# Length of queries and keys in the token stage: a sum onto all partitions and a wide root and inverse, in place of a narrow sum, a narrow root and a spread

## The chip, the core and the metric

The kernel runs on one core of a Trainium2 chip. The metric is the device time of one execution in microseconds, of which three are given for the kernel before. Engines are named as in the profile: PE is TensorE (matmul) and PEld its weight load, DVE is VectorE, ACT is ScalarE, POOL is GpSimd, SP is SyncE, whose queue issues most of the DMAs. Each engine takes its instructions in the order in which they were written for it, and waits at semaphores.

## The reference, cut to what matters

Two transformer layers are followed by a third block with a gated delta rule and sixteen experts. The change lies in that third block, where the tokens' queries, keys and values are made. There are 512 tokens, four heads and 128 features a head:

```python
def l2norm(x):
    xf = x.astype(jnp.float32)
    return xf * lax.rsqrt(jnp.sum(xf * xf, axis=-1, keepdims=True) + EPS)
...
    proj = h @ w_in
    (q, k, v), log_a, beta = deltanet_inputs(proj[..., :QKV_COLS], proj[..., QKV_COLS:STATE_COLS],
                                             conv_w, a_log, dt_bias)
    q = l2norm(q) * DN_HEAD_DIM ** -0.5
    k = l2norm(k)
    o, states = bidir_delta(q, k, v, log_a, beta, s0)
```

`deltanet_inputs` runs a convolution of four taps along the tokens over each feature and then silu. `l2norm` divides each token's 128 features of one head by their length.

## The kernel before, in words

The stage is the class `Mixer2`, "token stage" below. Activations lie transposed: 128 features on the partitions, 512 tokens along the free axis. Tile c (0 to 11) is one head of the queries (0 to 3), keys (4 to 7) or values (8 to 11). Tiles 0 to 7 are divided by their length, tiles 8 to 11 are not.

The stage's matmuls come in 20 items (`self.items`), each with half a block of `win2`. Items 0 to 3, 6 to 9 and 12 to 15 make tiles 0 to 3, 4 to 7 and 8 to 11, 24 matmuls of 512 columns each; items 4, 5, 10 and 11 make the gate and 16 to 19 the pool's input, 48 matmuls of 256 columns each. A product is taken in three parts, high by high, high by low and low by high, so ACT first rounds an item's weights ("split", line 490, CAST 128x1024) and DVE subtracts for the low part (line 264, TENSOR_TENSOR 128x1024). At step i, splits are made mostly for item i + 3.

The generator `steps` sets the order. All engines run through the same list of (name, number) and each does its part of a step, so the list is the order of every queue. Per step i:

- PE: item i, then "finish", then "csum" where they stand.
- ACT: copies the product out of its bank (line 840, `put_act`; for other items lines 280 and 3125), casts the next split, and in `conv_act` takes the tanh for the silu and, for tiles 0 to 7, the square.
- DVE: the low part of the split, "finish", then `conv_dve`: one TENSOR_SCALAR and three SCALAR_TENSOR_TENSOR for the taps, and after ACT's tanh one more for the silu.

"conv" of tile c stands at the item's own step from c = 2 on. Its first tap overwrites the buffer `ctmp[c % 2]`, which holds the squares of tile c - 2.

The length is found like this. "csum" of tile c: four matmuls, each with 128 tokens of the squares as weights and a column of ones, leave the sums with tokens on the partitions, 4 columns a tile, in bank 6. "root", once for four tiles: DVE adds the epsilon and takes the inverse of 128x16 numbers (line 885), ACT takes their root. "finish" of tile c: four matmuls with a column of the roots repeated 128 times as weights and the identity spread them over all partitions into bank 2 or 3, and DVE multiplies the tile by that bank (line 274, from PSUM). Csum stands at steps 2 to 5 and 8 to 11, root at steps 5 and 11, finish of tiles 0 to 3 at steps 6 to 9 and of tiles 4 to 7 at steps 12 to 15.

Between them stand "delta" 0 to 3 at steps 2 to 5 (narrow work on the decays; the last has 34 matmul records on PE), "gate" 0 to 3 at steps 11 to 14 (a tanh on ACT and one operation on DVE each), and at steps 14, 16 and 18 a CAST of 128x2048 on ACT for the pool (line 3013). The stage ends with transposes ("turn", line 388) and the pool's matmuls.

Of the kernel before, what the change touches and what calls it, by code (L numbers as in the profile page):

```python
# [11 lines left out]
ACT = mybir.ActivationFunctionType  # L12
# [10 lines left out]
EPS = 1e-6  # L23
# [229 lines left out]
def mm(e, out, l, r, start=True, stop=True):  # L253
    return e.h.matmul(out, l, r, start=start, stop=stop)  # L254
# [2613 lines left out]
class Mixer2(Conv):  # L2868


    def __init__(self, k):
        super().__init__(k, "mixb", "mixb")
        al = k.al
        k.reset()
        self.nt = 4
        self.qkf = al(4096)
        self.qT, self.kT = v3(self.qkf[:, 0:2048], 4), v3(self.qkf[:, 2048:4096], 4)
        self.gate, self.ab = v3(al(2048), 4), v3(al(64), 4)
        vTf, tmpf = al(2048), al(2048)
        self.vT = self.O = v3(vTf, 4)  # L2880
        self.poolT = v3(tmpf, 4)
        self.utf, self.rawf = al(2048), al(2064)
        self.ut, self.mT, raw = v3(self.utf, 4), v3(self.rawf[:, 0:2048], 4), v3(self.rawf, 4)
        self.poolw = al(512)
        self.uhi4 = k.fr(tmpf).rearrange("p (g t c) -> p t g c", g=4, t=4)
        self.ulo4 = k.fr(self.utf).rearrange("p (t g c) -> p t g c", g=4, t=4)
        self.inv = v3(k.b4f, 4)
        self.Kt, self.Vt = v3(k.low[:, 0:2048], 4), v3(k.low[:, 2048:4096], 4)
        self.units()
        self.hp = k.parts(k.hTf, k.low)  # L2890
        self.conv_init(raw, 512, [tmpf[:, 512 * i:512 * i + 512] for i in range(4)], 0,
                       lambda i: (self.qT, self.kT, self.vT)[i // 4][:, i % 4, :],
                       lambda i: (128.0 ** -0.5, 1.0, None)[i // 4])
        self.dma, self.dma_inv = k.count("in_poolw"), k.count("in_inv")
        self.items = []
        w = k.A["win2"]
        for blk, kind in ((0, "fm"), (1, "fm"), (6, "gate"), (2, "fm"), (3, "fm"), (7, "gate"), (4, "fm"), (5, "fm"),
                          (8, "ut"), (9, "ut")):
            self.add("fm" if kind == "fm" else "tok", w[blk], SLOT, (kind, blk))
        self.number()  # L2900
        self.last_gate = max(i for i, it in enumerate(self.items) if it.tag[0] == "gate")
        self.nbox = k.ring.reserve(4)
        self.bx = [v3(k.fr(k.ring.slot(self.nbox + g)), 4) for g in range(4)]
        self.ends = [(self.V, "O"), (self.S, ("mT", 3)), (self.P, ("pool", 3))]
# [8 lines left out]
    def steps(self):  # L2913
        yield from self.first()
        yield "norm", 0
        pend, fin = [], []
        for i, it in enumerate(self.items):
            open_ = [j for j in (i - 1, i) if j >= 0 and (self.items[j].kind == "tok" and not self.items[j].half) == (j < i)]
            for j in open_:
                if j < i and j + 3 < len(self.items):  # L2920
                    yield "split", j + 3
            yield "sum", i
            if i in open_ and i + 3 < len(self.items):
                yield "split", i + 3
            if i == 1:
                yield "small", 0
                yield "conv", 0
            elif i == 2:
                yield "small", 1
                yield "conv", 1  # L2930
            if 2 <= i < 6:
                yield "delta", i - 2
            if fin:
                yield "finish", fin.pop(0)
            if pend and pend[0][1] + 2 <= i:
                c = pend.pop(0)[0]
                yield "csum", c
                if c % 4 == 3:
                    yield "root", c // 4
                    fin = [c - 3, c - 2, c - 1, c]  # L2940
            if it.tag[0] == "fm":
                c = self.conv_of(i)
                if c > 1:
                    yield "conv", c
                if self.scale(c) is not None:
                    pend.append((c, i))
            g = i - 11
            if 0 <= g < 4:
                yield "gate", g
        for c in fin:  # L2950
            yield "finish", c
        for m in range(8):
            yield "turn", m
        yield "O", 0
        for g in range(4):
            yield "box", g
            if g:
                yield "pool", g - 1
        yield "pool", 3
# [5 lines left out]
    def tok_pe(self, e, i, bank, src, ready):  # L2965

        half = self.items[i].half
        for a in range(2):
            j = i - half + a
            hi, lo, _ = self.views(j)  # L2970
            e.wait_ge(self.lower(j).at(("lo", j)))
            for t in range(2):
                c = slice((2 * half + t) * 128, (2 * half + t) * 128 + 128)
                for k in range(4):
                    x = src(4 * a + k)
                    e.wait_ge(ready(4 * a + k))
                    p = mm3(e, bank[:, 256 * t:256 * t + 256], (x[0][:, c], x[1][:, c]), (hi[:, k, :], lo[:, k, :]),
                            a == 0 and t == 0 and k == 0, a == 1 and t == 1 and k == 3)
            p.then_inc(*self.P.tick((("half", "sum")[a], i)))

    def conv_of(self, i):
        it = self.items[i]
# [37 lines left out]
    def pe(self, e):  # L3020
        k, P, S, V, B = self.k, self.P, self.S, self.V, self.k.bank
        self.enter(e)
        for name, i in self.steps():
# [4 lines left out]
            elif name == "sum" and i > 1:  # L3028
                it = self.items[i]
                if it.kind == "fm":  # L3030
                    c = self.conv_of(i)
# [6 lines left out]
                        e.wait_ge(V.at(("ulo", old[-1])) if self.items[old[-1]].tag[0] == "ut" else S.at(("tok", old[-1])))  # L3038
                    self.tok_pe(e, i, B[it.half], self.hp, lambda c: V.at(("h", c)))
            elif name == "csum":  # L3040
                e.wait_ge(V.at("small_tr") if i < 4 else V.at(("cmean", i // 4 - 1)))
                self.csum_pe(e, i, B[6])
            elif name == "finish":
                if i >= 2:
                    e.wait_ge(V.at(("cfin", i - 2)))
                self.finish_pe(e, i, B[2 + i % 2])
            elif name == "small":
                if i:
                    self.small_tr_pe(e, B[6], 4)
                else:  # L3050
                    self.small_pe(e, B[7], 2, 512, self.hp)
            elif name == "delta":
                e.wait_ge(V.at("small"))
                self.delta.pe_step(e, self.delta.SETUP[i], 0)
            elif name == "turn":
                if i < 4:
                    e.wait_ge(V.at(("ulo", len(self.items) - 1)))
                else:
                    e.wait_ge(S.at(("raw", 11)))
                if i >= 6:  # L3060
                    e.wait_ge((S if i % 2 else V).at(("turn", i - 6)))
                src, _ = self.turn(i)
                for c in range(4):
                    e.wait_ge(self.conv_done(4 + 4 * (i // 4) + c))
                    p = k.tr(e, B[i % 6][:, c * 128:c * 128 + 128], src[c])
                p.then_inc(*P.tick(("turn", i)))
            elif name == "box":
                n = self.nbox + i
                a = 2 * (i % 2)
                e.wait_ge(S.at(("bx", i)), V.at(("ulo", len(self.items) - (3 if i < 2 else 1))))  # L3070
                if i >= 2:
                    e.wait_ge(S.at(("mT", i - 2)))
                else:
                    e.wait_ge(S.at(("turn", 7)), V.at(("turn", 6)))
                self.box_pe(e, i, B[a], self.bx[i]).then_inc(*P.tick(("box", i)))
                k.ring.released[n] = [(P, ("box", i))] + (self.delta.ends if i >= 2 else [])
            elif name == "pool":
                b = 2 * (i % 2) + 1
                e.wait_ge(S.at(("mT", i)), self.dma.at(0))
                if i >= 2:  # L3080
                    e.wait_ge(V.at(("pool", i - 2)))
                mm(e, B[b][:, :], self.poolw[:, i * 128:i * 128 + 128], self.mT[:, i, :]).then_inc(*P.tick(("pool", i)))
# [15 lines left out]
    def act(self, e):  # L3098
# [4 lines left out]
        for name, i in self.steps():  # L3103
# [22 lines left out]
                if i in (14, 16, 18):  # L3126
                    self.box_act(e, i // 2 - 7)
            elif name == "root":
                self.croot_act(e, i)
            elif name == "conv":  # L3130
                self.conv_act(e, i)
            elif name == "gate":
# [14 lines left out]
    def dve(self, e):  # L3147
        k, P, S, V, B = self.k, self.P, self.S, self.V, self.k.bank
        self.enter(e)
        e.h.memset(self.raw[:, :, 0:2], 0.0)  # L3150
        e.h.memset(self.raw[:, :, 514:516], 0.0).then_inc(*V.tick("zero"))
        for name, i in self.steps():
            if name == "split":
                self.split_dve(e, i)
            elif name == "norm":
# [3 lines left out]
                for c in range(9):  # L3159
# [5 lines left out]
                    if c:  # L3165
# [1 line left out]
                        e.wait_ge(S.at(("nhi", c - 1)))  # L3167
                        stt(e, lo, k.two[(c - 1) % 2], k.MOD[:, c - 1, 0:1], hi.bitcast(F32), ALU.add, ALU.subtract).then_inc(
                            *V.tick(("h", c - 1)))
            elif name == "root":  # L3170
                self.croot_dve(e, i, B[6])
            elif name == "finish":
                self.finish_dve(e, i, B[2 + i % 2])
            elif name == "delta":
                e.wait_ge(V.at("small_tr"))
                self.delta.dve_step(e, self.delta.SETUP[i], 0)
# [884 lines left out]
```

## Time and profile before

| | before |
|---|---|
| three executions, us | 2977.16, 2980.09, 2974.94; median 2977.16 |
| profiled execution, us | 2971.13 |
| its span, us | 2969.3 |
| mean granted clock of PE | 0.989 |
| busy share of PE, DVE, ACT, POOL | 96%, 55%, 34%, 9% |
| HBM read | 436.40 MB |

The span is what the hardware profiler recorded from the first to the last instruction; the execution's own time is 1.8 us longer. A matmul that waits in PE's pipe counts as busy, so 96% doesn't say that PE is at its peak. The share of an engine is a mean over stages with different limits. The token stage takes from 2133 to 2299 us of the span.

### The profile page before, as it was taken

What the parts mean: (1) busy time and instruction counts of PE and PEld (TensorE: products, weight loads), DVE (VectorE), ACT (ScalarE), POOL (GpSimd) and SP (SyncE); (2) the same over time, 40 slices, a digit from 0 to 9 for tenths busy, and PEclk for the clock granted to TensorE, in tenths of its full rate; (3) what the DMA queues carried; (4) which work ended last, traced back from release to release, by engine and by line L of the source; (5) the groups of instructions that cost most, each with busy time, mean ns of one, the idle gap of its engine ahead of it and who ended that gap; (6) DMA issues with size and microseconds to landing.
All of it is one profiled execution on the core that took longest, in us unless ns stands there. A gap on an engine that the chain in (4) does not pass through costs nothing.

```text
span 2969.3 us, 41268 instructions
## 1 busy us (share of the span) xinstructions
PE 2838.8 (96%) x17052; PEld 2193.0 (74%) x17052; DVE 1624.5 (55%) x3042; ACT 1012.9 (34%) x2075; POOL 258.3 (9%) x284
## 2 busy tenths in 40 slices
PE   8999999999999999999999999999999897998888
PEld 6888877888888888888887888888788885332323
DVE  6876686465655565555585565454555764221213
ACT  4222363563332343232353552222344552000002
POOL 0000012230000000000022330000000730000000
PEclk9999999999999999999999999999999998999999
DMA  5454421112232222222221112222322028999997
GB/s 204 181 207 162 181 102 57 44 72 99 94 116 89 99 86 93 83 82 86 86 86 44 57 67 104 100 85 93 110 72 85 3 102 324 413 424 425 425 425 323
DMA packets 59868, 444.58 MB, mean 150 GB/s; under 512 B 6816, under 2 KB 7072, under 8 KB 23072
## 3 DMA queue, kind: packets, MB, share of 16 engines
q1 hardware_dynamic: 56544, 430.12, 37.7%
q0 software_dynamic: 1696, 6.55, 0.6%
q10 hardware_dynamic: 1440, 5.25, 0.5%
q8 instruction: 135, 2.21, 0.3%
q14 instruction: 53, 0.43, 0.0%
HBM read 436.40 MB, written 5.51 MB: 149 GB/s over the span
## 4 chain that ended last, share of the span: by engine, by line
PE 78%; DMA 10%; DVE 8%; ACT 2%; issue 1%; POOL 1%; SPq 0%; ACTq 0%; DVEq 0%; POOLq 0%
PE ps L254 77%; DMA b<-in_eg 5%; DVE b L264 3%; DMA b<-in_ed 2%; DVE b L274 2%; PE ps L388 1%; DMA b<-in_eu 1%; DVE b L800 1%; ACT b L280 1%; DMA b<-in_wu 1%; ACT b L490 1%; POOL b L264 1%; DVE b L2336 0%; DMA b<-in_wd 0%; DMA b<-in_wg 0%
## 5 line engine op out<-in xcount | busy, mean ns | idle before, releaser
L254 PE MATMUL ps<-b,b 128*128 128x512 f32 (+10 forms) x13874 | 2648.6, 378 | 82.8 <-DVE b L274 19.8
L254 PEld LDWEIGHTS ps<-b,b 128*128 128x128 f32 (+4 forms) x13874 | 2016.4, 177 | 678.4 <-issue 225.0
L264 DVE TENSOR_TENSOR b<-b,b 128x512 f32<-128x512 f32 (+8 forms) x755 | 626.3, 836 | 292.0 <-ACT b L490 213.7
L490 ACT CAST b<-b 128x1024 fp32r<-128x1024 f32 (+2 forms) x408 | 392.2, 963 | 414.6 <-PE ps L254 324.1
L264 DVE TENSOR_TENSOR b<-ps,b 128x64 f32<-128x64 f32 (+6 forms) x437 | 174.6, 420 | 226.7 <-PE ps L254 188.3
L264 POOL TENSOR_TENSOR b<-b,b 128x1024 fp32r<-128x1024 f32 (+8 forms) x159 | 183.2, 1171 | 1083.4 <-ACT b L2413 505.5
L280 ACT ACTIVATE b<-b 128x512 f32<-128x512 f32 (+7 forms) x304 | 155.7, 522 | 232.2 <-DVE b L274 172.4
L274 DVE SCALAR_TENSOR_TENSOR b<-ps,b,b 128x128 f32<-128x128 f32 (+4 forms) x224 | 110.6, 540 | 218.3 <-ACT b L280 118.7
L264 DVE TENSOR_TENSOR b<-b,ps 128x512 f32<-128x512 f32 (+1 forms) x114 | 76.8, 678 | 231.6 <-PE ps L254 230.8
L254 PE MATMUL ps<-b 64*64 64x64 f32 (+10 forms) x2704 | 174.9, 264 | 21.1 <-DVE b L264 10.7
L274 DVE SCALAR_TENSOR_TENSOR b<-b,b 128x512 f32<-128x512 f32 (+6 forms) x296 | 176.4, 610 | 27.3 <-ACT b L280 23.7
L1678 ACT CAST b<-b 128x512 fp32r<-128x512 f32 x88 | 54.6, 620 | 379.5 <-DVE b L264 379.5
L254 PEld LDWEIGHTS ps<-b 64*64 64x64 f32 (+4 forms) x2704 | 146.0, 155 | 41.4 <-issue 14.8
L274 DVE SCALAR_TENSOR_TENSOR b<-ps,b 128x512 f32<-128x512 f32 (+1 forms) x144 | 97.2, 678 | 140.1 <-PE ps L254 128.5
L280 ACT ACTIVATE b<-b,b 128x128 f32<-128x128 f32 (+3 forms) x204 | 101.1, 538 | 138.5 <-DVE b L274 70.1
L274 DVE SCALAR_TENSOR_TENSOR b<-b,b,b 128x512 fp32r<-128x512 f32 (+4 forms) x176 | 124.5, 722 | 23.6 <-ACT b L280 20.7
L280 ACT ACTIVATE b<-ps 128x512 f32<-128x512 f32 (+3 forms) x102 | 40.0, 420 | 276.5 <-PE ps L254 276.4
L388 PEld LDWEIGHTS ps<-b,b 128*128 128x128 f32 (+2 forms) x474 | 54.1, 146 | 45.0 <-issue 15.0
L388 PE MATMUL ps<-b,b 128*128 128x128 f32 (+2 forms) x474 | 72.1, 289 | 15.6 <-DVE b L264 6.2
L1336 POOL MEMSET b<- 128x128 f32 x12 | 1.9, 205 | 956.3 <-PE ps L254 542.9
L800 DVE CUSTOM_DVE_ANT_0 b<-b,b,b 128x1024 f32<-128x1024 f32 x64 | 80.5, 1277 | 0.0
L280 ACT ACTIVATE b<-ps,b 128x64 f32<-128x64 f32 (+2 forms) x70 | 34.7, 511 | 126.0 <-PE ps L254 121.2
(120 smaller groups left out, 612.2 us busy)
## 6 DMA issues: line engine op xcount, KB each, us to landing
b<-in_eu SPq DMA_DIRECT2D x28, 2048.0 KB, 35.5
b<-in_wg SPq DMA_DIRECT2D x44, 1024.0 KB, 4.8
b<-in_wu SPq DMA_DIRECT2D x44, 1024.0 KB, 4.8
b<-in_win SPq DMA_DIRECT2D x40, 1024.0 KB, 4.8
b<-in_ed SPq DMA_DIRECT2D x20, 2048.0 KB, 34.0
b<-in_wd SPq DMA_DIRECT2D x48, 768.0 KB, 4.3
b<-in_eg SPq DMA_DIRECT2D x29, 1024.0 KB, 28.6
b<-in_eg SPq DMA_DIRECT2D x14, 2048.0 KB, 35.1
```

Source lines behind the costliest of these rows:

```text
L254: return e.h.matmul(out, l, r, start=start, stop=stop)
L264: return e.h.tensor_tensor(out, a, b, op)
L274: return e.h.scalar_tensor_tensor(out, a, s, b, op0, op1)
L280: return e.h.activation(out, a, f, bias=bias, scale=scale)
L388: return e.h.transpose(out, i, self.K["ident"][0:n, 0:n])
L490: e.h.copy(hi, src).then_inc(*self.S.tick(("hi", i)))
L800: p = e.h.tensor_tensor_reduce(self.tmp[:, 1024 * c:1024 * c + 1024], w, self.crow[:, 1024 * c:1024 * c + 1024], 0.5, k.col("bmod", i), AL ...
L1336: z = e.h.memset(t, 0.0)
L1678: e.h.copy(self.ahi[:, f - self.f0[grp], :], t).then_inc(*S.tick(("ahi", f)))
```

## The change

In the token stage alone, the squares of a tile (128x512) become the moving side of one matmul whose weights are the 128x128 matrix of ones, so each token's sum stands at once on all 128 partitions of a bank. The bank is one of 2, 3 and 6 in turn. Once for two tiles ACT takes the root of the whole bank, 128x512, from PSUM into the same bank, with the epsilon as its bias. "Finish" has no matmuls any more: DVE takes the inverse of 128x512 in the bank and multiplies the tile by it. Csum 3 and later ones wait until the tile three before is finished, because its bank is theirs. The stage for the context (the class `Context`) keeps the old way.

```diff
+        self.eps = al(8)[:, 0:1]
...
                 yield "csum", c
-                if c % 4 == 3:
-                    yield "root", c // 4
-                    fin = [c - 3, c - 2, c - 1, c]
+                if c % 2:
+                    yield "root", c // 2
+                    fin += [c - 1, c]
...
+    def sumbank(self, c):
+        return self.k.bank[(2, 3, 6)[c % 3]]
...
             elif name == "csum":
-                e.wait_ge(V.at("small_tr") if i < 4 else V.at(("cmean", i // 4 - 1)))
-                self.csum_pe(e, i, B[6])
-            elif name == "finish":
-                if i >= 2:
-                    e.wait_ge(V.at(("cfin", i - 2)))
-                self.finish_pe(e, i, B[2 + i % 2])
+                e.wait_ge(V.at("small_tr"), S.at(("csq", i)))
+                if i > 2:
+                    e.wait_ge(V.at(("cfin", i - 3)))
+                mm(e, self.sumbank(i)[:, :], k.K["one"], self.ctmp[i % 2]).then_inc(*P.tick(("csum", i)))
...
             elif name == "root":
-                self.croot_act(e, i)
+                for c in (2 * i, 2 * i + 1):
+                    e.wait_ge(P.at(("csum", c)), V.at("eps"))
+                    b = self.sumbank(c)[:, :]
+                    act(e, b, b, ACT.Sqrt, self.eps).then_inc(*S.tick(("croot", c)))
...
+        e.h.memset(self.eps, EPS).then_inc(*V.tick("eps"))
...
-            elif name == "root":
-                self.croot_dve(e, i, B[6])
             elif name == "finish":
-                self.finish_dve(e, i, B[2 + i % 2])
+                d = self.dst(i)
+                e.wait_ge(S.at(("croot", i)))
+                b = self.sumbank(i)[:, :]
+                e.h.reciprocal(b, b).then_inc(*V.tick(("cinv", i)))
+                e.wait_ge(V.at(("cinv", i)))
+                stt(e, d, d, self.scale(i), b, ALU.mult, ALU.mult).then_inc(*V.tick(("cfin", i)))
```

The list of steps is now: csum at steps 2 to 5 and 8 to 11 as before; root 0, 1, 2, 3 at steps 3, 5, 9, 11; finish of tiles 0 to 7 at steps 4, 5, 6, 7, 10, 11, 12, 13.

On DVE, this is the piece of the difference from the end of step 4 to the start of step 7 (b_339 holds queries and keys, b_343 the buffers `ctmp`, b_345 the items' products, b_349 to b_354 the split weights, b_56 the taps):

```order
+L3180 RECIPROCAL ps<-ps 128x512
+L274 SCALAR_TENSOR_TENSOR b_339<-b_339,ps 128x512
 L264 TENSOR_TENSOR b_352<-b_51,b_349 128x1024
 L264 TENSOR_TENSOR b_353<-b_52,b_350 128x1024
-L264 TENSOR_TENSOR b_370<-b_363,b_371 128x32
-L269 TENSOR_SCALAR b_357<-ps 128x16
-L885 RECIPROCAL b_357<-b_357 128x16
+L264 TENSOR_TENSOR b_371<-b_364,b_372 128x32
+L3180 RECIPROCAL ps<-ps 128x512
+L274 SCALAR_TENSOR_TENSOR b_339<-b_339,ps 128x512
 L264 TENSOR_TENSOR b_354<-b_52,b_351 128x1024
+L3180 RECIPROCAL ps<-ps 128x512
```

Finish of tiles 0 and 1 now stands at steps 4 and 5, finish of tile 2 at step 6, each with a wide inverse ahead of its product; the narrow pair for four tiles is gone.

On ACT, this is the piece of the difference at step 9, from the split's CAST to the tanh and the square of tile 7 (b_339 and b_343 as above, b_358 the epsilon):

```order
 L490 CAST b_351<-b_50 128x1024
+L280 ACT_TABLE_LOAD
+L280 ACTIVATE ps<-ps,b_358 128x512 x2
+L280 ACT_TABLE_LOAD
 L280 ACTIVATE b_343<-b_343 128x512
 L280 ACTIVATE b_343<-b_339 128x512
```

Two wide roots stand between the cast and the tanh, with a table load on either side. At step 3 the same instructions are new ahead of tile 3's tanh.

On PE, the piece of the difference between items 8 and 9, at step 8 (b_54 holds the constants, b_357 the roots; b_355 and b_356 are the activations, b_350, b_351 and b_353 split weights):

```order
 L254 MATMUL ps<-b_356,b_350 128x512
 L254 MATMUL ps<-b_355,b_353 128x512
-L254 MATMUL ps<-b_54,b_357 128x128 x4
-L254 MATMUL ps<-b_54,b_343 128x1 x4
+L254 MATMUL ps<-b_343,b_54 128x512
 L254 MATMUL ps<-b_355,b_351 128x512
 L254 MATMUL ps<-b_356,b_351 128x512
```

The eight narrow matmuls of finish and csum between two items have become one of 512 columns.

## Rows read from the trace of the kernel before

**Rows 1.** The page: busy time by engine, and the chain that ended last by engine.

```profile
PE 2838.8 (96%) x17052; PEld 2193.0 (74%) x17052; DVE 1624.5 (55%) x3042; ACT 1012.9 (34%) x2075; POOL 258.3 (9%) x284
...
PE 78%; DMA 10%; DVE 8%; ACT 2%; issue 1%; POOL 1%; SPq 0%; ACTq 0%; DVEq 0%; POOLq 0%
```

**Rows 2.** The chain in order of time, token stage: start, length, what.

```profile
2165.29 73.84 PE ps L254 x466
2239.16 0.59 ACT b L840
...
2240.72 1.23 DVE b L264
2241.95 0.59 DVE b L274
...
2274.90 8.91 PE ps L254 x72
```

**Rows 3.** ACT in order of time: start, length; idle before and its releaser in brackets.

```profile
2183.98 0.63 ACT L280 ACTIVATE b<-b 128x512 f32<-128x512 f32 x1 [3.22 <-DVE b L274]
...
2198.62 0.59 ACT L840 COPY b<-ps 128x512 f32<-128x512 f32 x1 [6.12 <-PE ps L254]
...
2206.73 0.57 ACT L840 COPY b<-ps 128x512 f32<-128x512 f32 x1
...
2236.21 1.28 ACT L280 ACT_TABLE_LOAD   x1
2237.50 0.63 ACT L280 ACTIVATE b<-b 128x512 f32<-128x512 f32 x1
...
2246.40 0.57 ACT L840 COPY b<-ps 128x512 f32<-128x512 f32 x1
...
2253.62 0.57 ACT L840 COPY b<-ps 128x512 f32<-128x512 f32 x1
...
2262.65 0.57 ACT L840 COPY b<-ps 128x512 f32<-128x512 f32 x1
...
2270.26 0.59 ACT L3125 CAST b<-ps 128x512 fp32r<-128x512 f32 x1 [0.81 <-DVE b L274]
```

**Rows 4.** DVE in order of time, the same columns.

```profile
2186.93 0.18 DVE L269 TENSOR_SCALAR b<-b 128x32 f32<-128x32 f32 x1
...
2191.47 0.17 DVE L269 TENSOR_SCALAR b<-ps 128x16 f32<-128x16 f32 x1 [0.36 <-PE ps L254]
...
2200.19 1.23 DVE L264 TENSOR_TENSOR b<-b,b 128x1024 fp32r<-128x1024 f32 x1 [8.26 <-ACT b L490]
2201.33 0.68 DVE L274 SCALAR_TENSOR_TENSOR b<-b,ps 128x512 f32<-128x512 f32 x1
```

**Rows 5.** Lines 885 and 2651, the inverses: ns min/median/max, first and last start, forms.

```profile
L885 DVE RECIPROCAL b<-b x3: 203/253/253, 881.8 to 2235.7; 128x16 f32<-128x16 f32 x2, 128x8 f32<-128x8 f32 x1
...
L2651 DVE RECIPROCAL b<-b x2: 553/553/553, 544.7 to 1647.3; 128x64 f32<-128x64 f32 x2
```

**Rows 6.** PE's groups by form, five stretches from 2190, 2231, 2231, 2198.6, 2297: us, mean ns.

```profile
L254 PE MATMUL ps<-b,b 128*128 128x512 f32 x24 | 7.3, 472 | 0.0
...
L254 PE MATMUL ps<-b,b 128*128 128x512 f32 x24 | 5.7, 394 | 0.0
...
L254 PE MATMUL ps<-b,b 128*128 128x1 f32 x8 | 0.9, 240 | 0.0
...
L254 PE MATMUL ps<-b,b 128*128 128x128 f32 x16 | 2.1, 274 | 0.0
...
L254 PE MATMUL ps<-b,b 128*128 128x512 f32 x5 | 2.2, 569 | 0.0
```

**Rows 7.** Stretches: us, PE, PEld, DVE, ACT, POOL busy, granted clock, DMA, GB/s.

```profile
2130.00:2140.00 10.00, 4.92 (x21) 4.03 (x19) 5.70 (x12) 4.74 (x7) 0.00 (x0) 0.66 0.63 236
```

**Rows 8.** SP's queue: the DMAs behind the token stage, start and length.

```profile
2290.84 140.54 SPq L158 DMA_DIRECT2D b<-in_wout  x4
2431.43 0.43 SPq L196 DMA_DIRECT2D b<-in_ed  x1
```

## The prediction

> **What bounds the kernel now.** I read the page first, then the chain that ended last in order of time, then ACT and DVE through the token stage. The page says that PE is busy 96% and holds 78% of the chain [rows 1], which invites the thought that any matmul saved is time saved. The token stage shows two different limits. From 2165 to 2239 the chain is PE alone, 73.84 us, which is items 3 to 12. From 2239.16, the copy of item 12's product, to 2274.90 it goes round ACT and DVE: copy, cast, low part, finish's product, taps, tanh, copy [rows 2]. One such round is 7.2 us at steps 12 and 13, 9.0 at step 14 (with the wide cast) and 7.6 at step 15, read from one copy to the next, up to 2270.26 [rows 2, 3]. In the first stretch the same round takes 2206.73 - 2198.62 = 8.1 us a step, with no idle time ahead of the second copy [rows 3]. So PE is named by the chain there, but ACT and DVE have no slack to speak of: whatever is put into a round at step 6 or later must soon be paid.
>
> The hole is earlier. DVE stands idle for 8.26 us before 2200.19 [rows 4] and ACT for 6.12 us before 2198.62 [rows 3]. Both wait for item 6.
>
> **What the change takes away.** Finish had four matmuls that the trace shows as 8 records; 16 records take 2.1 us [rows 6], so 1.05 us a tile. Four finishes lie in PE's stretch: 4.2 us. Csum's eight narrow records took 0.9 us. The new csum is one matmul of 512 columns whose numbers are plain fp32. Its price is bounded by an item's matmul, 5.7 / 24 = 0.24 us, and by two records at 2.2 / 5 = 0.44 us each, from the stretch with the pool's fp32 products [rows 6]. I take 0.9 us, the upper end, since those are of its kind. Csum changes nothing then. DVE also loses 0.4 us of narrow work at steps 5 and 11, beside other work.
>
> **What it adds on DVE.** Eight inverses of 128x512. No row has one so wide. The narrow ones give a straight line: 128x8 takes 203 ns, 128x16 takes 253, 128x64 takes 553 [rows 5]. That is 6.25 ns for each element of a partition above 153 ns. At 512 it is 153 + 3200 = 3.35 us. Bounds: a DVE pass over 128x512 from PSUM takes 0.68 us [rows 4], which it would be at one element a time like the product; and twice the line's slope would be 6.6 us. I take the line, since it is the same operation and its three points lie on it; reading and writing PSUM may add a little, and with the wait between inverse and product I put 3.4 us on each.
>
> The Trainium skill (VectorE: DVE Perf Modes, "First, the fixed hardware budget") says that the inverse is divided iteratively with a repeat count of 8. At one repeat a cycle of 0.96 GHz this is an estimate of 8.3 ns an element, 4.4 us in all. The rows show 6.25 ns, so the measured slope decides here, and the page's price is a rival below.
>
> **What it adds on ACT.** Four more table loads and eight wide roots for two narrow ones. A load is 1.28 us and the next ACTIVATE starts at its end, 2237.50 after 2236.21 [rows 3]. A wide root is priced like the copy of a bank or a tanh, 0.6 to 0.7 us [rows 3]. Step 3 has load, two roots, load: 1.28 + 1.4 + 1.28 = 3.9 us where ACT waits 3.22 us for DVE ahead of the tanh at 2183.98 [rows 3], so all of step 3 and 4 moves back by 0.6 us. Step 9 has the same 3.9 us, beside DVE's low part and taps, which take 1.2 + 0.4 + 2.3 us: hidden, with nothing to spare. If DVE's cover were gone it would cost 3.9. The loads at steps 5 and 11 were there before.
>
> **The steps on the path.**
> 1. Step 4. DVE ends delta 2 at 2187.1 [rows 4], now 0.6 later. Finish 0 then runs 3.4 + 0.7 us, to 2191.8. Csum 3 waits for it, because the two share bank 2. Before, csum 3 had ended at 2191.5 [rows 4]; now it ends at 2192.7. Behind it on PE stands item 6: +1.2 us.
> 2. Step 5. Finish 1 starts after two low parts at about 2194 and ends near 2198.3, inside the hole (DVE was idle until 2200.19). Cost nothing. Without the hole it would be 4.1 us.
> 3. Steps 6 and 7. Item 6's copy is at 2199.8. The round of 8.1 us already holds a finish, so it becomes 11.5, twice: the copies of items 7 and 8 come at 2211.3 and 2222.8. Item 9 needs tile 5's copy only, but csum 5 behind it needs tile 5's squares, 2222.7, so PE stands idle ahead of item 10. PE is no longer the limit, and the 4.2 us of finish that it saves are idle time.
> 4. Steps 8 and 9. No finish stands here: 8.1 - 0.6 = 7.5 us each. Tile 7's silu ends at about 2237.2.
> 5. Step 10. Finish 4 follows at once, 4.1 us, to 2241.3. Csum 7 waits for it (bank 3), to 2242.2, and behind csum 7 stands item 12 on PE, 5.7 us: 2247.9. PE has waited some 3 us by then. After a wait of 3 us ahead of the first items, the granted clock of the stretch was 0.66 [rows 7], and 24 matmuls at the fallen clock (level 1.2 GHz for part of the time) took 7.3 instead of 5.7 us [rows 6]. I add 1.6: 2249.5, where it was 2239.16. So +10.3 us up to here.
> 6. Steps 12 and 13. Rounds 7.2 + 3.4 = 10.6 us, twice. Step 14: 9.0 - 0.6 = 8.4. Step 15: 7.6 - 0.6 = 7.0. Item 16's cast, 2270.26 before, comes at 2249.5 + 36.6 = 2286.1: +15.9 us.
>
> From there on all is as before. The transposes and the pool follow item 19. The last of the four loads of in_wout is let go at 2431, and the experts' first load comes right behind it on SP [rows 8], so the experts' DMA stream, which bounds the end of the kernel, moves back with the stage and hides none of it. Against the profiled execution's own time of 2971.13 us (span 2969.3) the sum is 2987.0. That execution was 6 us below the median of 2977.16; I forecast against the median: 2977.2 + 15.9 = 2993 us. A measurement of this kernel can tell about 0.2%, 6 us, from no change.
>
> **Rivals.**
> - *A dearer inverse* (the page's price, or PSUM adds to the line). At 4.4 us, six inverses are on the path (tiles 0, 2, 3, 4, 6, 7): + 6 x 1.05 = 6.3, or 2999 us. For it: nothing measured is so wide. Against it: three points on a line.
> - *Table switches cost a drain.* The Trainium skill (ScalarE: Activation LUTs, "What ACT_TABLE_LOAD costs") gives about 1.38 us of drain beside each load of 1.28. The load at 2236.21 is followed at once [rows 3], so this trace doesn't show one ahead of the next ACTIVATE. Worked out by rows: were each load at steps 3 and 9 as long again, 2.6 us at each place would be bare and the time 2998.
> - *A cheap inverse* (the other side). If the wide form runs like the product from the bank, 0.7 us, rounds grow by 0.7 at four steps and shrink by 0.6 at four others, PE loses 4 us of finish that the rounds don't let it use, and the end is where it was: 2977 us, no change. It decides below some 1.5 us an inverse. Against it stand the same three points.
> - *PE is the limit and DVE's work lies beside it*, as the chain's 73.84 us would have it. Then 4.2 us of finish go, and 0.6 us each from the four rounds behind 2239: 6.6 us, 2970.6 us, faster. Against it: the copy at 2206.73 with no wait for PE.
>
> **How the numbers follow.** My forecast with its own range of 2985 to 2998 has 0.68. The dearer inverse and the drain together 0.18, the cheap inverse 0.08, PE as the limit 0.06. Of the slower ones a few in a hundred may end below 6 us, if DVE overlaps better than I think. So faster 0.05, within 0.2% 0.09, slower 0.86. The range of 2982 to 3003 holds the forecast and the dearer cases and leaves out the two cheap ones.
>
> **What would show it.** The inverse at line 3180: 3.3 to 3.5 us each. ACT's copies of items 6, 7 and 8 spaced by 11.5 us, then 7.5. PE with idle time ahead of csum 5 and csum 7. Item 12's copy about 10 us later, the cast of item 16 about 16 us later, and the stages behind unchanged in length. The prediction fails if the inverse is not on the line, if the hole ahead of 2200 doesn't hold two finishes, or if PE's clock falls for longer than one item.

## The result, and the profile after

The changed kernel is slower. Over seven executions its median is 2993.25 us against 2977.16 us before; the ratio is 1.0043 with a 95% interval of 1.003 to 1.0056, that is 12.8 us with an interval of 9 to 17. Two of its seven executions took 9965 and 12796 us, which nothing here explains; the ratio leaves them out, and the median of the other five is 2990.5.

The page of the changed kernel, its span, its engines' busy time and the chain by engine, beside [rows 1]:

```profile
span 2993.5 us, 41065 instructions
PE 2844.0 (95%) x16940; PEld 2191.1 (73%) x16940; DVE 1650.4 (55%) x3047; ACT 1022.8 (34%) x2085; POOL 256.7 (9%) x284
...
PE 76%; DMA 10%; DVE 9%; ACT 3%; issue 1%; POOL 1%; ACTq 0%; SPq 0%; DVEq 0%; POOLq 0%
```

DVE has 25.9 us more to do, which is the eight inverses (26.9 us) less the narrow work; the page doesn't say where that hurts. The rows of the new line of code (line 3180: ns min/median/max, first and last start) do, and so does DVE in order of time around the first waits (start, length, idle time before):

```profile
L3180 DVE RECIPROCAL ps<-ps x8: 3356/3357/3359, 2193.6 to 2267.6; 128x512 f32<-128x512 f32 x8
```

```profile
2193.56 3.36 DVE L3180 RECIPROCAL ps<-ps 128x512 f32<-128x512 f32 x1
...
2203.32 0.69 DVE L274 SCALAR_TENSOR_TENSOR b<-b,ps 128x512 f32<-128x512 f32 x1
2207.67 1.23 DVE L264 TENSOR_TENSOR b<-b,b 128x1024 fp32r<-128x1024 f32 x1 [3.66 <-ACT b L490]
2208.81 3.36 DVE L3180 RECIPROCAL ps<-ps 128x512 f32<-128x512 f32 x1
...
2243.43 3.36 DVE L3180 RECIPROCAL ps<-ps 128x512 f32<-128x512 f32 x1
2246.82 0.69 DVE L274 SCALAR_TENSOR_TENSOR b<-b,ps 128x512 f32<-128x512 f32 x1
...
2253.69 0.68 DVE L274 SCALAR_TENSOR_TENSOR b<-b,b 128x512 f32<-128x512 f32 x1
2255.83 1.23 DVE L264 TENSOR_TENSOR b<-b,b 128x1024 fp32r<-128x1024 f32 x1 [1.46 <-ACT b L490]
```

An inverse takes 3.357 us. That of tile 1 fits in the hole: its product ends at 2204.0 and DVE still waits 3.66 us before 2207.67 (8.26 us in the kernel before, [rows 4]). Tile 0's lies ahead of csum 3, for which see step 1 in the section on the prediction. From tile 2 on the inverses stand in the round. ACT shows it in the distance of its copies, and at step 3 the new roots with their loads:

```profile
2186.67 1.28 ACT L280 ACT_TABLE_LOAD   x1
2187.96 1.24 ACT L280 ACTIVATE ps<-ps,b 128x512 f32<-128x512 f32 x2
2189.22 1.28 ACT L280 ACT_TABLE_LOAD   x1
2190.51 0.63 ACT L280 ACTIVATE b<-b 128x512 f32<-128x512 f32 x1
...
2206.10 0.59 ACT L840 COPY b<-ps 128x512 f32<-128x512 f32 x1 [5.58 <-PE ps L254]
...
2217.61 0.57 ACT L840 COPY b<-ps 128x512 f32<-128x512 f32 x1
...
2229.09 0.57 ACT L840 COPY b<-ps 128x512 f32<-128x512 f32 x1
...
2236.59 0.57 ACT L840 COPY b<-ps 128x512 f32<-128x512 f32 x1
...
2254.27 0.59 ACT L840 COPY b<-ps 128x512 f32<-128x512 f32 x1 [2.75 <-PE ps L254]
...
2290.96 0.59 ACT L3127 CAST b<-ps 128x512 fp32r<-128x512 f32 x1 [0.81 <-DVE b L274]
```

Items 6, 7 and 8 are 11.51 and 11.48 us apart, where it was 8.11 [rows 3], and item 9 follows after 7.50. PE, which had run through this stretch, now waits in it (PE in order of time):

```profile
2229.24 14.82 PE L254 MATMUL ps<-b,b 128*128 128x512 f32 x100 [4.88 <-ACT b L280]
2247.65 17.46 PE L254 MATMUL ps<-b,b 128*128 128x512 f32 x74 [3.59 <-DVE b L274]
```

The first wait is csum 5 for tile 5's squares, the second csum 7 for tile 4's finish. The chain's PE piece of 73.84 us [rows 2] is gone, and the inverse is a link of its own. The chain holds six of the eight, those of tiles 0, 2, 3, 4, 6 and 7; this is tile 2's (the chain in order of time):

```profile
2206.69 0.95 ACT b L490
2207.67 1.23 DVE b L264
2208.89 3.29 DVE ps L3180
2212.20 0.69 DVE b L274
```

To compare kernels I took the starts of five instructions: item 0's copy (line 840, the first in the stage), item 6's copy, item 12's copy (the ninth), item 16's cast, and the first transposed copy on DVE. The four differences, in us, from the traces:

| kernel | item 0 to 6 | 6 to 12 | 12 to 16 | 16 to transposed | sum |
|---|---|---|---|---|---|
| before | 46.15 | 40.54 | 31.10 | 15.63 | 133.42 |
| changed | 47.74 | 48.17 | 36.69 | 16.73 | 149.33 |

The stage grew by 15.9 us. The profiled span grew by 24.2: item 0's copy stands 5.9 us later already (2152.47 and 2158.36), in code that is the same but for one small memset that sets the epsilon, and 2.4 us came behind the stage. These parts I don't count as the change's; the last section comes back to them.

### The profile page after: what moved, and what is told of

It reads as the page before. It is cut to its first block, busy times and chain, and to the rows that moved or that the text cites. A ratio compares the mean times of both kernels' runs of the same rounds, so it can differ in the third digit from the quotient of the medians.

```text
span 2993.5 us, 41065 instructions
## 1 busy us (share of the span) xinstructions
PE 2844.0 (95%) x16940; PEld 2191.1 (73%) x16940; DVE 1650.4 (55%) x3047; ACT 1022.8 (34%) x2085; POOL 256.7 (9%) x284
## 4 chain that ended last, share of the span: by engine, by line
PE 76%; DMA 10%; DVE 9%; ACT 3%; issue 1%; POOL 1%; ACTq 0%; SPq 0%; DVEq 0%; POOLq 0%
PE ps L254 75%; DMA b<-in_eg 5%; DVE b L274 3%; DVE b L264 3%; DMA b<-in_ed 2%; ACT b L280 1%; PE ps L388 1%; DMA b<-in_eu 1%; DVE b L800 1%; ACT b L490 1%; DMA b<-in_wu 1%; DVE ps L3180 1%; POOL b L264 1%; DVE b L269 0%; DVE b L2336 0%
## 5 line engine op out<-in xcount | busy, mean ns | idle before, releaser
L254 PE MATMUL ps<-b,b 128*128 128x512 f32 (+7 forms) x13762 | 2655.5, 381 | 99.6 <-DVE b L274 23.8
L254 PEld LDWEIGHTS ps<-b,b 128*128 128x128 f32 (+3 forms) x13762 | 2015.9, 178 | 702.7 <-issue 232.5
L280 ACT ACTIVATE b<-b 128x512 f32<-128x512 f32 (+8 forms) x302 | 155.3, 523 | 236.6 <-DVE b L274 176.5
L254 PE MATMUL ps<-b 64*64 64x64 f32 (+10 forms) x2704 | 174.2, 262 | 22.4 <-DVE b L264 10.7
## 6 DMA issues: line engine op xcount, KB each, us to landing
b<-in_eg SPq DMA_DIRECT2D x14, 2048.0 KB, 35.2
```

The source lines that it names most:

```text
L280: return e.h.activation(out, a, f, bias=bias, scale=scale)
```

## Experiments

All of them start from the changed kernel unless said otherwise. Ratios are to the kernel before, run beside it on the same chip. The stage's parts are read as in the table above, each from one profiled execution.

### A cheap pass in place of each inverse

```diff
-                e.h.reciprocal(b, b).then_inc(*V.tick(("cinv", i)))
+                ts(e, b, b, 0.0, ALU.mult, 0.03, ALU.add).then_inc(*V.tick(("cinv", i)))
```

> The changed kernel, but in place of each of the eight wide inverses DVE makes one pass of the same 128x512 in the same bank that writes the constant 0.03 (the inverse is left out, so queries and keys are scaled by a constant). Everything else stays: the wide csum, the wide roots, the table loads, the waits, the places. Theory (the inverse's length in the ACT and DVE round, six of eight on the path): a pass should take 0.7 us instead of 3.36; the stage from item 0's copy to item 16's cast falls from 132.6 us by 5 x 2.7 (tiles 2, 3, 4, 6, 7) and by up to 1.6 for tile 0, less what PE then limits, to 118 to 120 us (before: 117.8), and the whole to 2976 to 2980 us, 13 to 16 us under the changed kernel. Rival (the roots, their table loads and the wide csum on the path): the stage stays above 128 us and the whole within 5 us of the changed kernel. Rival (a cheap inverse would be no change): this run is that case itself, and should end within 0.2% of the kernel before.

Measured: 2978.31 us, ratio 1.0004 (0.999 to 1.0018). Item 0's copy and item 16's cast on ACT:

```profile
2162.86 0.59 ACT L840 COPY b<-ps 128x512 f32<-128x512 f32 x1 [4.61 <-PE ps L254]
...
2282.06 0.59 ACT L3127 CAST b<-ps 128x512 fp32r<-128x512 f32 x1 [0.81 <-DVE b L274]
```

119.2 us lie between them, within the 118 to 120 expected. With the wide sum, the wide roots and all table loads in place, 13.4 of the 14.8 us lost up to item 16's cast are gone, and the ratio can't be told from 1. A pass takes 0.69 us for 3.36, so 13.4 us are just five inverses' worth. All of it came behind item 6: from item 0 to 6 the stage still takes 47.70 us (changed 47.74, before 46.15), so this run doesn't show that tile 0's inverse costs anything. The rival that blames ACT or the fp32 matmul falls, but for the 1.4 us that are left.

### The cheap pass at tiles 1 and 5 only

```diff
-                e.h.reciprocal(b, b).then_inc(*V.tick(("cinv", i)))
+                (ts(e, b, b, 0.0, ALU.mult, 0.03, ALU.add) if i in (1, 5) else e.h.reciprocal(b, b)).then_inc(*V.tick(("cinv", i)))
```

> As the run before this one, but the constant pass stands in for the inverse only at tiles 1 and 5 (so these two tiles are scaled by a constant). 2 x 2.7 us less work on DVE. Theory of the path: tile 1's finish lies in the hole ahead of item 6's low part and tile 5's ends 1.5 us before ACT's next cast is there, so neither is on the path: the stage stays at 132.6 us within 0.5 and the whole does not move. Rival (DVE's load as such sets the time, each inverse counts a share): the stage shortens by 2 x 15 / 8, 3.7 us.

Measured: 2993.27 us, ratio 1.0058 (1.0039 to 1.0076). No gain from 5.3 us less work on DVE, where the rival (each inverse counts a share) wanted 3.7 us. The rounds from item 12 to 16 take 36.69 us, the same as in the changed kernel to the hundredth. The stage up to item 16's cast missed the expectation, though; it took 134.0 us against 132.6 (expected: within 0.5). Item 6 to 12 took 1.6 us more, and the matmuls of item 12 met a lower clock. The first row is this run's, with 0.83, the second the changed kernel's, with 1.00 (us, busy PE, PEld, DVE, ACT, POOL, granted clock, DMA, GB/s):

```profile
2240.00:2250.00 10.00, 8.74 (x30) 6.75 (x31) 5.34 (x7) 5.62 (x8) 0.00 (x0) 0.83 0.30 107
```

```profile
2247.00:2255.00 8.00, 7.35 (x31) 5.76 (x32) 7.34 (x6) 5.19 (x8) 0.00 (x0) 1.00 0.39 133
```

### No root, no table loads

```diff
-                    act(e, b, b, ACT.Sqrt, self.eps).then_inc(*S.tick(("croot", c)))
+                    act(e, b, b, ACT.Identity, self.eps).then_inc(*S.tick(("croot", c)))
```

> The changed kernel with the root left out: ACT passes the bank through the identity (plus epsilon) instead of the square root, 128x512 in place as before, so no table loads stand around it (so queries and keys are divided by the square of their length). Inverses stay. Theory of the path: the loads and roots are hidden but for 0.6 us at step 3, so the stage falls from 132.6 us by 0.6 to 1.5 and the whole by 1 us, not to be told from the changed kernel. Rival (table switches with a drain on the path at steps 3 and 9): the stage falls by 4 us or more, to 128 or less.

Measured: 2990.99 us, ratio 1.0049 (1.0034 to 1.0065), not to be told from the changed kernel. The round of step 9, where roots and loads stood beside the taps, is unchanged at 7.5 us (from the copy of item 9 at 2239.78 to that of item 10 at 2247.27). ACT and PE in order of time:

```profile
2239.78 0.57 ACT L840 COPY b<-ps 128x512 f32<-128x512 f32 x1
...
2247.27 0.58 ACT L280 ACTIVATE b<-ps 128x512 f32<-128x512 f32 x1
...
2250.85 11.36 PE L254 MATMUL ps<-b,b 128*128 128x512 f32 x35 [3.35 <-ACT ps L280]
...
2260.20 0.59 ACT L840 COPY b<-ps 128x512 f32<-128x512 f32 x1 [6.06 <-PE ps L254]
```

So the loads at step 9 are hidden and carry no further drain onto the path. Those of step 3 show their 0.6 us: tile 3's tanh starts 32.15 us after item 0's copy in the changed kernel, 31.54 here and 31.51 before. Item 6's copy doesn't come sooner by it (47.82 us). The stage itself missed the expectation: not 0.6 to 1.5 us shorter, but 135.4 us up to item 16's cast, 2.8 longer. Csum 7 and item 12 took 9.35 us here, from 2250.85 to the copy at 2260.20, for 6.6 in the changed kernel, with a clock of 0.73 from 2250 to 2262.

### The finishes of tiles 4 to 7 late

```diff
-            if fin:
+            if fin and not 10 <= i < 16:
                 yield "finish", fin.pop(0)
...
-        return self.k.bank[(2, 3, 6)[c % 3]]
+        return self.k.bank[(2, 3, 6, 2, 3, 6, 2, 7)[c]]
...
-                if i > 2:
+                if 2 < i < 7:
                     e.wait_ge(V.at(("cfin", i - 3)))
```

> The changed kernel with all its work, but the finishes of tiles 4 to 7 (inverse and product) moved from steps 10 to 13 to steps 16 to 19; the sums of tiles 3 to 7 lie in banks 2, 3, 6, 2 and 7, so that csum 7 waits for no finish. Same number of inverses, same DVE work. Theory of the path: csum 7 no longer waits 3.6 us for finish 4, and steps 12 and 13 lose 4.0 us each: item 16's cast comes 11 to 12 us sooner (stage 121 us). The four inverses then fill DVE's waits of 2, 4.3 and 5.1 us behind item 16, 11.4 us for 16.4 us of work, so 5 us come back ahead of the transposes: about 7 us less than the changed kernel up to the first transposed copy, whole about 2985 to 2987. Rival (DVE's load as such): no change. Rival (the wait at csum 7 alone): 3.6 us less.

Measured: 2990.69 us, ratio 1.0041 (1.0026 to 1.0056). Up to item 16's cast the stage takes 121.8 us (expected 121), up to the first transposed copy 143.1, 6.3 less than in the changed kernel (expected 7). The same eight inverses, 11 us less at one point and 6 at the next: the place decides. Behind item 16, DVE and PE show the rest:

```profile
2294.78 3.36 DVE L3180 RECIPROCAL ps<-ps 128x512 f32<-128x512 f32 x1
...
2298.17 0.69 DVE L274 SCALAR_TENSOR_TENSOR b<-b,ps 128x512 f32<-128x512 f32 x1
2298.91 6.08 PE L388 MATMUL ps<-b,b 128*128 128x128 f32 x29 [3.45 <-DVE b L274]
```

The transposes wait 3.45 us for the last finish, then they run at a low clock (0.60 from 2298 to 2306) and take over 6 us instead of 3.7. That gives back another 2.4 us, which I had not expected. The whole missed the 2985 to 2987 us: by the ratio it can't be told from the changed kernel, and from item 0's copy to the end of the span it is 2.3 us shorter.

### The same banks, no finish moved

```diff
-        return self.k.bank[(2, 3, 6)[c % 3]]
+        return self.k.bank[(2, 3, 6, 2, 3, 6, 2, 7)[c]]
...
-                if i > 2:
+                if 2 < i < 7:
                     e.wait_ge(V.at(("cfin", i - 3)))
```

> The changed kernel, all work and all places the same; only the banks of the sums are 2, 3, 6, 2, 3, 6, 2, 7, so that csum 7 does not wait for finish 4. Theory of the path: PE's wait of 3.6 us ahead of csum 7 goes and item 12's copy comes 3.5 us sooner, at 92.4 after item 0's copy (changed 95.9), but DVE is then busy with finish 5 and the gate until 96.0, so its low part for item 15 starts only 1.4 us sooner: item 16's cast at 131.2 (changed 132.6). Where the clock falls at item 12 both are longer by up to 2.7. Rival (the wait at csum 7 is worth its length): 129.0.

Measured: 2989.52 us, ratio 1.0042 (1.0026 to 1.0058). From item 6 to 12 it took 45.3 us (changed 48.2), from 12 to 16 38.0 (36.7): 1.6 us less together, where 1.4 was expected and 3.6 would have been the wait's length. The whole can't be told from the changed kernel. DVE in order of time at steps 11 and 12:

```profile
2249.14 0.69 DVE L274 SCALAR_TENSOR_TENSOR b<-b,ps 128x512 f32<-128x512 f32 x1
2249.75 0.69 DVE L274 SCALAR_TENSOR_TENSOR b<-b,b 128x512 f32<-128x512 f32 x1
2250.35 1.22 DVE L264 TENSOR_TENSOR b<-b,b 128x1024 fp32r<-128x1024 f32 x1
```

No idle time stands ahead of the low part: it queues behind tile 5's inverse and the gate. The wait of PE that the trace named was worth less than half its length. Item 0 to 6 took 1.2 us more than in the changed kernel (49.0), at a clock of 0.66 from 2190 to 2203, so item 16's cast came at 132.3 us and not at the 131.2 expected.

### Logarithm and exponential on ACT in place of root and inverse

```diff
-                    act(e, b, b, ACT.Sqrt, self.eps).then_inc(*S.tick(("croot", c)))
+                    act(e, b, b, ACT.Ln, self.eps).then_inc(*S.tick(("cln", c)))
+                for c in (2 * i, 2 * i + 1):
+                    e.wait_ge(S.at(("cln", c)))
+                    b = self.sumbank(c)[:, :]
+                    act(e, b, b, ACT.Exp, scale=-0.5).then_inc(*S.tick(("croot", c)))
...
-                e.h.reciprocal(b, b).then_inc(*V.tick(("cinv", i)))
-                e.wait_ge(V.at(("cinv", i)))
```

> The changed kernel's order and sums, but the inverse of the root is made on ACT alone as exp(-0.5 ln(sum + eps)), two passes of 128x512 in the bank instead of one root; DVE does the product only. All work is done. Two more passes of 0.62 us a pair of tiles on ACT, the same number of table switches (ln, then exp and tanh share one). Theory of the path: step 3 loses 1.9 us against the kernel before (5 us of roots and loads for 3.2 of cover), step 9 about 1.1, csum 7 waits little for finish 4; PE no longer has the finishes and the rounds of steps 14 and 15 lose 0.6 each. Stage from item 0's copy to item 16's cast 117 to 118.5 us (before 117.8, changed 132.6), whole within 0.2% of the kernel before. Rival (the table switches and wide passes on ACT are what costs, not the inverse): the stage stays at 125 or more.

Measured: 2978.18 us, ratio 1.0002 (0.9991 to 1.0013). Item 16's cast comes 117.4 us after item 0's copy (expected 117 to 118.5). Behind it the same 96 matmuls took 14.3 us, 12.2 before, at a clock of 0.82 from 2277 to 2296. All of the work is done here, so the loss of the changed kernel is not the price of the wide sum, but of where and by whom its inverse is taken.

### The same, moved to where ACT and DVE wait

```diff
-                if c % 2:
-                    yield "root", c // 2
-                    fin += [c - 1, c]
+                if c == 3:
+                    yield "root", 0
+                    for c in range(4):
+                        yield "finish", c
+            if i == 17:
+                yield "root", 1
+                for c in range(4, 8):
+                    yield "finish", c
...
-        return self.k.bank[(2, 3, 6)[c % 3]]
+        return self.k.bank[(2, 3, 6, 7)[c % 4]]
```

(Not shown: the two lines that took one finish a step are gone; root takes four tiles at a time with ln and exp, and the inverse is gone from finish; csum 3 waits until delta has read bank 7, and from csum 4 on each waits for the finish four tiles before.)

> As the run with ln and exp, all work done, and moved to where engines wait: the root of tiles 0 to 3 in one batch at step 5, in ACT's wait of 6 us for item 6, with their four products in DVE's wait of 8 us; the root and products of tiles 4 to 7 behind item 17. Sums in banks 2, 3, 6 and 7. Theory of the path: no round of steps 6 to 9 and 12 to 15 has a finish, each 7.5 or 6.6 us; PE, without finishes, brings item 12 about 2 us sooner; item 16's cast 4 to 5 us sooner than in the kernel before (113 to 114 us after item 0's copy), about 0.7 of which comes back before the transposes: first transposed copy at 129 to 130.5 (before 133.4). Whole about 4 us under the kernel before, ratio 0.9985, which five rounds may just not tell from one. Rival (something else in the wide form costs, such as PE's one fp32 matmul or a fallen clock after the changed mix): no gain in the stage.

Measured: 2974.22 us over 12 executions, ratio 0.9992 (0.998 to 1.0004). The stage is 4.7 us shorter than before, 128.7 us up to the first transposed copy (expected 129 to 130.5), and item 16's cast comes after 112.0 us (expected 113 to 114). ACT and DVE in order of time at step 5 and at items 6 and 7:

```profile
2196.00 2.40 ACT L280 ACTIVATE ps<-ps,b 128x512 f32<-128x512 f32 x4
...
2199.71 2.05 ACT L280 ACTIVATE ps<-ps 128x512 f32<-128x512 f32 x4
2200.32 2.48 DVE L274 SCALAR_TENSOR_TENSOR b<-b,ps 128x512 f32<-128x512 f32 x4 [5.26 <-ACT ps L280]
2203.64 0.59 ACT L840 COPY b<-ps 128x512 f32<-128x512 f32 x1 [1.88 <-PE ps L254]
...
2211.15 0.57 ACT L840 COPY b<-ps 128x512 f32<-128x512 f32 x1
```

Eight ACT passes and four products pass in the waits for item 6, and ACT still waits 1.88 us. The round is 7.5 us. By the ratios the whole is 15 us under the changed kernel, but its gain over the kernel before, 2.4 us by the ratio and 4.7 by the stage, can't be told from none: the interval holds 1.

### The kernel before, with its finishes of tiles 4 to 7 late

```diff
-            if fin:
+            if fin and not 12 <= i < 16:
                 yield "finish", fin.pop(0)
```

> The kernel before, narrow sums and all, with only the finishes of tiles 4 to 7 moved from steps 12 to 15 to steps 16 to 19. All work is done. Theory of the path: the four rounds behind item 12 lose 0.6 us each, item 16's cast at 115.4 us after item 0's copy (before 117.8); but finish's 8 records on PE now stand between the last items, where PE is the limit: 1 us and up to 0.7 of product come back, first transposed copy at 132 to 133 (before 133.4). Whole unchanged within what can be measured. It says whether the wide form is needed for the gain of the moved one. Rival (finish is hidden wherever it stands): item 16's cast stays at 117.8.

Measured: 2975.01 us, ratio 0.9989 (0.9977 to 1.0001). The rounds from item 12 to 16 take 28.7 us for 31.1, the 2.4 us expected, and 1.2 come back behind item 16. The cast itself stands at 118.4 us instead of the expected 115.4, because items 0 to 6 took 49.2 us instead of 46.2, at a clock of 0.80 from 2190 to 2207. From item 6 to the first transposed copy this gains 1.2 us, where the moved wide form gains 5.1. The two moves are not the same, though: here the finishes of tiles 0 to 3 stay at steps 6 to 9, and 3.8 of the 5.1 us lie in items 6 to 12. No run moved the narrow form's first four, so whether the wide form is needed for that gain stays open.

All parts together, in us; the last but one column runs from item 0's copy to the end of the span:

| kernel | item 0 to 6 | 6 to 12 | 12 to 16 | 16 to transposed | item 0 to end | ratio |
|---|---|---|---|---|---|---|
| before | 46.15 | 40.54 | 31.10 | 15.63 | 816.8 | 1 |
| changed | 47.74 | 48.17 | 36.69 | 16.73 | 835.1 | 1.0043 |
| cheap pass, all tiles | 47.70 | 40.15 | 31.35 | 15.63 | 818.6 | 1.0004 |
| cheap pass, tiles 1 and 5 | 47.58 | 49.73 | 36.69 | 15.63 | 836.1 | 1.0058 |
| no root | 47.82 | 50.91 | 36.68 | 15.63 | 836.4 | 1.0049 |
| late finishes | 47.42 | 45.65 | 28.70 | 21.30 | 832.8 | 1.0041 |
| same banks | 48.98 | 45.33 | 37.96 | 15.64 | 834.2 | 1.0042 |
| ln and exp | 47.22 | 40.28 | 29.89 | 17.76 | 820.7 | 1.0002 |
| ln and exp, moved | 46.48 | 36.77 | 28.71 | 16.73 | 813.4 | 0.9992 |
| before, late finishes | 49.16 | 40.54 | 28.69 | 16.79 | 818.8 | 0.9989 |

The cheap pass at all tiles, which only shortens the inverse, takes back 16.5 of the 18.3 us that the changed kernel loses behind item 0's copy; what the clock did to either is not separated in these two numbers.

## Why the prediction was right, step by step

- **The price of the inverse** was the term that everything hung on, drawn out from three narrow rows to one eight times as wide. 3.35 us was worked out, 3.357 measured. The repeat count of 8 that the Trainium skill states (VectorE: DVE Perf Modes, "First, the fixed hardware budget"), taken at a cycle each, gave an estimate of 4.4; the measurement decides against that reading.
- **Step 1**, csum 3 behind finish 0: +1.2 predicted, 47.74 - 46.15 = +1.6 measured. The order is right: finish 0 ran from 35.2 to 39.3 us after item 0's copy, as worked out, csum 3 started at 39.4, and the chain goes through both. But the agreement of the numbers is no proof of the cost. PE had waited 0.43 us for it (2.27 us in the run with the same banks), and with the cheap pass, where PE had no such wait, this part was as long. The kernel before and its late form have the same code up to item 6 and took 46.15 and 49.16 us. Two wide roots took 1.24 us together where I had put 1.4.
- **Step 2**, finish 1 in the hole: predicted to cost nothing, and it cost nothing (3.66 us of idle time are left behind it; taking its inverse away gained nothing).
- **Step 3**, rounds of 11.5 us: 11.51 and 11.48. PE waited for csum 5, 4.88 us.
- **Step 4**, 7.5 us a round, with the root of step 9 hidden: 7.50, and ACT's tanh there waited 0.2 us for DVE.
- **Step 5**, finish 4, csum 7 and item 12: the order of waits was right. The 1.6 us added for a fallen clock was mis-sized for this execution. From csum 7's start at 2247.65 to the copy at 2254.27 took 6.6 us, at full clock; so items 6 to 12 took 48.2 us where the prediction had 49.7. The same work did meet a lower clock in two other runs and took 1.6 and 2.7 us more, so 1.6 was within what can happen and wrong as a certainty. Its ground was weak too: the row with 0.66 [rows 7] ends before item 0's matmuls start at 2140.58 (right behind that start, from 2140 to 2144, the trace has 0.56), and the 7.3 us [rows 6] are item 6's, ahead of which PE had not waited at all.
- **Step 6**, 36.6 us from item 12 to 16: 36.69. Item 16's cast came 14.8 us later than before counted from item 0's copy, where 15.9 was predicted.
- **"From there on all is as before"**: not quite. Behind item 16, 96 matmuls took 13.3 us instead of 12.2 at a clock that fell to 0.63 for 4 us: +1.1. That the stage up to the first transposed copy grew by just the 15.9 us that were predicted up to item 16's cast is in part luck: the clock's term came at another place. What the inverse surely accounts for is less, the 7.6 and 5.6 us between items 6 and 16, 13.2 us, which the cheap pass took away again.
- **The rivals.** The cheap inverse was right in what it would give (1.0004 for a cheap pass) and wrong in its price. PE as the limit is refuted by PE's new waits. The drain at a table switch (the Trainium skill, ScalarE: Activation LUTs, "What ACT_TABLE_LOAD costs") doesn't show: after the load at 2189.22 the next ACTIVATE starts at 2190.51, the ACTIVATEs ahead of that load end at 2189.20, and without loads the round of step 9 is no shorter. The dearer inverse falls with the 3.357 us.

What I had not separated: the whole's median moved by 16.1 us and the ratio by 12.8, with an interval 8 us wide. The median of 2993.25 is that of all seven; the ratio's five have 2990.5. That it fell on the 2993 of the forecast is luck, and says less than the stage's parts do.

## What to carry to other kernels

Price a DVE inverse by its elements from the narrow ones in the same trace before making it wide: an inverse that is cheap on 16 columns costs 3.4 us on 512, so spread the result instead of the sum, or take it on an engine that has room. Where the chain names one engine for a long stretch, look at the spacing of the others' rounds: two engines that hand each other the work of a step in a round as long as PE's, 8.1 us here, leave nothing to hide in, though each is idle for a part of it (ACT up to 4.65 us a wait, while DVE works). And before a wait is removed, ask what its engine's partner is doing meanwhile; here 3.6 us of PE's waiting were worth 1.6. An inverse of 3.4 us in the round cost its length, and the same one in a wait, as tile 1's, cost nothing.

## What the runs showed of the hardware that was not expected

The granted clock moves stages from one execution to the next. Ahead of item 0's copy all these kernels run the same code but for the memset, yet the copy stands between 2152.14 and 2162.86 us in ten profiled executions, with a mean clock of the whole between 0.980 and 0.989. The clock goes with it: summing up to 2150 us, in windows of 50 us, the share of the clock that was not granted gives 5 us before, 11 in the changed kernel, 14 without the root and 15 with the cheap pass, and their copies come at 2152.47, 2158.36, 2161.47 and 2162.86. Items 0 to 6 took 46.2 to 49.2 us, and the 26 or so matmuls of csum 7 and item 12 took 6.6 us at full clock in one run and 9.35 at 0.73 in another, each after a wait of PE of 3.4 to 3.6 us. The first of these spreads, 10.7 us, is larger than 0.2% of this kernel (6 us); the other two are about 3 us each. The clock also falls without any wait: in the kernel before, where PE runs through from 2165.29, it is 0.57 from 2191 to 2195. A stage's parts that ACT and DVE pace (36.68, 36.69 and 36.69 us in three kernels) repeat to a hundredth, so effects of a few us are best read there. What makes the clock fall in one run and not in another stays open; no run here was made for it.
